# Cross-attention of a fused two-block model: softmax units, query chunks and value products dealt out in another order

## The chip, the core and the metric

The kernel runs on one core of a Trainium2 chip. The metric is device time in microseconds for one execution. The engines that matter are PE (TensorE, matmuls), DVE (VectorE), ACT (ScalarE), POOL (GpSimd) and SP, which only issues weight transfers. Each engine takes its instructions in the order in which the program writes them, and waits on semaphores where it needs another engine's result.

## The reference

A first block of two layers (gated recurrence, sparse attention) is followed by a second block of two layers (convolution, retention, spatial gating, cross-attention, gated feed-forward). The change lies in the second block's cross-attention, which each of its two layers runs once, on 512 tokens, 256 memory rows and a model width of 1024:

```python
def cross_attention(h, mm, wq, wk, wv, wo):
    q = (h @ wq).reshape(B, S, XA_HEADS, XA_HEAD_DIM)      # 4 heads of 256
    k = (mm @ wk).reshape(B, M, XA_HEADS, XA_HEAD_DIM)
    v = (mm @ wv).reshape(B, M, XA_HEADS, XA_HEAD_DIM)
    s = jnp.einsum('bshd,bmhd->bhsm', q, k).astype(jnp.float32) * (XA_HEAD_DIM ** -0.5)
    p = jax.nn.softmax(s, axis=-1).astype(v.dtype)
    o = jnp.einsum('bhsm,bmhd->bshd', p, v).reshape(B, S, D_MODEL)
    return o @ wo
```

## The kernel before

Every float32 product is made of three matmuls on split operands: high by high, low by high, high by low. Weights come in chunks of 128 x 1024 numbers through a ring of four slots: SP loads a chunk into `raw`, ACT rounds it to `whi` (three chunks ahead of its use), POOL subtracts for `wlo`, and PE uses both. Results in PSUM banks are split in the same way: ACT writes the high part, DVE subtracts for the low part and so frees the bank.

`steps_two()` writes out by hand the list of steps of a layer. All engines walk through this one list, each doing its own share of every step, so the list fixes the order of the work on each engine. The steps of the cross-attention are:

- a *query chunk*, `("fm", "xq", i, ..)`: 24 matmuls of 512 columns for 128 of the 1024 columns of q. DVE scales the result into `tA` or `tB`, ACT copies that to `qx8`, DVE subtracts for its low part. Head h needs chunks 2h and 2h+1.
- a *value chunk*, `("tm", "xv0" or "xv1", i, ..)`: 12 matmuls of 512 columns. Four of them fill banks 2 and 7 (`xv1`), and only the last one has its result copied out.
- a *unit*, `("xatt", hh, qt)`: u = 4 hh + qt, 16 in all. On PE it holds `scores(v)`, six matmuls of 256 columns, for those units v that `scored_in(u)` names, and then `probs_turn(u + 1)`, two transposes. So scores run ahead, by as much as `scored_to(u)` says. Between the scores and the transposes of a unit stand DVE's maximum (`greatest`), ACT's exponential and sum (`probs`) and DVE's reciprocal and scaling of `Px` (`shares`). After the transposes, ACT and DVE copy them, split, into `PxT` (`turned` on ACT); this frees the transposes' bank for the unit after the next.
- a *value product*, `("xout", hh)`: 12 matmuls of 512 columns on `PxT` and `vx`.
- an *output chunk*, `("tm", "xw0", i, ..)`: 24 matmuls of 512 columns, the first two on the results of heads 0 and 1, the next two on those of heads 2 and 3.

`groups_two` says which PSUM banks the results of a step take, in turns.

Before the change, query chunks 0 to 3 stand ahead of the scores, chunks 4 to 7 behind units 2, 3, 6 and 7, the four value chunks behind units 0 to 3, and the value product of a head directly behind its last unit (and the chunk there). Units 8 to 15 have no weight chunk between them. Scores run two units ahead up to unit 3, three at unit 4, four from unit 5.

Of the kernel before, what the change touches and what calls it, by code (L numbers as in the profile page):

```python
# [36 lines left out]
TT = T // P  # L37
KD = D // P
# [18 lines left out]
XH, XD = 4, 256  # L57
# [136 lines left out]
def tm(kind, *a, **k):  # L194
    specs = tm_chunks(*a, **k)
    return [("tm", kind, i, len(specs), s) for i, s in enumerate(specs)]
# [186 lines left out]
def steps_two():  # L383
# [27 lines left out]
    xv1 = tm("xv1", "xa_v_2", 512, 512)  # L411
    xq = fm("xq", "xa_q_2", 0, KD)
    s += [("sums", "xa")] + xv0[:2] + [("rows", "xa")] + xq[:2] + xv0[2:3] + xq[2:3] + xv0[3:] + xq[3:4]
    for hh in range(XH):
        for qt in range(TT):
            s += [("xatt", hh, qt)] + (xv1[qt:qt + 1] if hh == 0 else [])
            s += xq[2 + 2 * hh + qt:3 + 2 * hh + qt] if qt >= 2 else []
        s += [("xout", hh)]
    xw1 = tm("xw1", "xa_o_2", 512, 512)
    s += tm("xw0", "xa_o_2", 0, 512) + xw1[:2] + [("turn_low", "ffn")] + xw1[2:]  # L420
    up = [x for f in range(FT) for x in (("fm", "u", f, ("w1_2", 0, KD, f * P, P)), ("fm", "w", f, ("w3_2", 0, KD, f * P, P)))]
# [12 lines left out]
def scored_to(u):  # L434


    return min(u + (2 if u < 4 else 3 if u == 4 else 4), XH * TT - 1)


def scored_in(u):  # L440
    return range(scored_to(u - 1) + 1 if u else 0, scored_to(u) + 1)


def groups_two(step):
    kind = step[0]
# [27 lines left out]
    if kind == "xatt":  # L473
        hh, qt = step[1:]
        return [(("xs", *divmod(u, TT)), (0, 1) if u < 6 else (2, 7, 0, 1)) for u in scored_in(hh * TT + qt)] + [(("xp", hh, qt), (3, 4))]
    if kind == "xout":
        return [(("xo", step[1], i), (5, 6)) for i in range(2)]
    return []


def build(nc, d, out, counts):
# [3 lines left out]
    with ExitStack() as ctx:  # L485
# [175 lines left out]
        ffn = ExitStack()  # L661
# [1116 lines left out]
        def tensor_two(pe, l):  # L1778
# [214 lines left out]
            def probs_turn(u):  # L1993
                name = ("xp", *divmod(u, TT))
                pe.wait_ge(*px_ready.at(l, u + 1))
                turn(name, MT, lambda i: Px[:, u % 4, i * P:(i + 1) * P])

            def step_xatt(step):
                hh, qt = step[1:]
                u = hh * TT + qt  # L2000
                if u == 0:
                    pe.wait_ge(*G.evacuated(("xk", KD - 1), l))
                for v in scored_in(u):
                    scores(v)
                    if v == 1:
                        probs_turn(0)
                if u + 1 < XH * TT:
                    probs_turn(u + 1)

            def step_xout(step):  # L2010
# [4 lines left out]
                for i in range(2):  # L2015
                    name, cols = ("xo", hh, i), slice(hh * XD + i * P, hh * XD + (i + 1) * P)
                    pe.wait_ge(*G.free(name, l))
                    for m in range(MT):
# [7 lines left out]
                     "ret_out": step_ret_out, "ret_turn": step_ret_turn, "sg_w": step_sg_w, "sg_mix": step_sg_mix,  # L2026
                     "sg_turn": step_sg_turn, "mg_turn": step_mg_turn, "xatt": step_xatt, "xout": step_xout}
            for step in steps2:
# [12 lines left out]
        def scalar_two(act, l):  # L2041
# [201 lines left out]
            def turned(u):  # L2243
                hh, qt = divmod(u, TT)
                name = ("xp", hh, qt)
                hi(PxT[:, hh % 2, 0, :, qt * P:(qt + 1) * P], name, G.ps(name)[:, 0:MEM].rearrange("p (m q) -> p m q", m=MT))

            def step_xatt(step):
                hh, qt = step[1:]
                u = hh * TT + qt  # L2250
                for v in scored_in(u):
                    if v == u + 2 or (v > 1 and v == scored_in(u)[0]):
                        turned(u)
                    probs(v)
                if not len(scored_in(u)):
                    turned(u)

            def step_xout(step):
                for i in range(2):
# [4 lines left out]
                     "ret_pair": step_ret_pair, "ret_out": step_ret_out, "ret_turn": step_ret_turn, "sg_w": step_sg_w, "sg_norm": step_sg_norm,  # L2264
                     "sg_turn": step_sg_turn, "mg_turn": step_mg_turn, "xatt": step_xatt, "xout": step_xout}
            for step in steps2:
# [6 lines left out]
        def vector_two(dve, l):  # L2273
# [285 lines left out]
            def shares(u):  # L2559
# [4 lines left out]
                ts(Px[:, u % 4, :], Px[:, u % 4, :], recx[:, c], None, ALU.mult).then_inc(*px_ready.up())  # L2564

            def step_xatt(step):
                hh, qt = step[1:]
                u = hh * TT + qt
                for v in scored_in(u):
                    if v > 1:  # L2570
                        shares(v - 1)
                    greatest(v)
                    if v == 1:
                        shares(0)
                if scored_to(u) == XH * TT - 1 and len(scored_in(u)):
                    shares(XH * TT - 1)
                at = (slice(None), slice(None), slice(qt * P, (qt + 1) * P))
                lo(PxT[:, hh % 2, 1][at], ("xp", hh, qt), PxT[:, hh % 2, 0][at], src=G.ps(("xp", hh, qt))[:, 0:MEM].rearrange("p (m q) -> p m q", m=MT))

            def step_xout(step):  # L2580
                for i in range(2):
# [3 lines left out]
                    else:  # L2585
# [4 lines left out]
                     "ret_out": step_ret_out, "ret_turn": step_ret_turn, "sg_w": step_sg_w, "sg_norm": step_sg_norm,  # L2590
                     "sg_mix": step_sg_mix, "sg_turn": step_sg_turn, "mg_turn": step_mg_turn, "xatt": step_xatt, "xout": step_xout}
            for step in steps2:
# [277 lines left out]
```

## Time and profile before

| what | value |
|---|---|
| time, median of 3 runs | 2967.58 us (2965.24 to 2969.01) |
| span of the profiled execution | 2966.5 us |
| PE busy | 2781.2 us, 94% |
| PE weight loads busy | 2312.4 us, 78% |
| ACT busy | 1283.9 us, 43% |
| DVE busy | 1225.9 us, 41% |
| POOL busy | 1157.0 us, 39% |
| mean granted TensorE clock | 0.971 |

The times are those of whole executions. The profile describes one further execution, whose own time is known only as its span from the first to the last instruction, 2966.5 us; it lies 1.1 us under the median of the timed runs and within their spread. In the rows below, the granted clock (PEclk) is a share of 2.4 GHz: 1.00 is the upper level and 0.50, 1.2 GHz, the lower. Starts are in us from the span's start. A busy time is what an engine worked in a stretch; the rest of the stretch it waited.

### The profile page before, as it was taken

What the parts mean: (1) busy time and instruction counts of PE and PEld (TensorE: products, weight loads), DVE (VectorE), ACT (ScalarE), POOL (GpSimd) and SP (SyncE); (2) the same over time, 40 slices, a digit from 0 to 9 for tenths busy, and PEclk for the clock granted to TensorE, in tenths of its full rate; (3) what the DMA queues carried; (4) which work ended last, traced back from release to release, by engine and by line L of the source; (5) the groups of instructions that cost most, each with busy time, mean ns of one, the idle gap of its engine ahead of it and who ended that gap; (6) DMA issues with size and microseconds to landing.
All of it is one profiled execution on the core that took longest, in us unless ns stands there. A gap on an engine that the chain in (4) does not pass through costs nothing.

```text
span 2966.5 us, 40477 instructions
## 1 busy us (share of the span) xinstructions
PE 2781.2 (94%) x13636; PEld 2312.4 (78%) x13636; DVE 1225.9 (41%) x2186; ACT 1283.9 (43%) x2191; POOL 1157.0 (39%) x537
## 2 busy tenths in 40 slices
PE   8989799998979998999998999999899999999998
PEld 6778668887856886788877888888688787788887
DVE  4766762476585234424222331313443423232132
ACT  4543754554374452444443432424254443253243
POOL 4323344331334442334442444444234453244442
PEclk9999899999989998999999999999899999999999
DMA  5213003321300231233331333333123333233332
GB/s 145 71 45 79 29 14 93 88 68 46 84 22 17 92 109 57 79 93 93 114 107 57 93 93 96 96 100 110 50 82 96 100 111 96 64 93 99 93 94 99
DMA packets 269778, 242.32 MB, mean 82 GB/s; under 512 B 29376, under 2 KB 201600, under 8 KB 269568
## 3 DMA queue, kind: packets, MB, share of 16 engines
q1 hardware_dynamic: 266672, 235.12, 27.1%
q10 hardware_dynamic: 2896, 4.52, 0.5%
q8 instruction: 118, 1.93, 0.3%
q14 instruction: 92, 0.75, 0.1%
HBM read 237.51 MB, written 2.10 MB: 81 GB/s over the span
## 4 chain that ended last, share of the span: by engine, by line
issue 46%; POOL 26%; PE 25%; DVE 1%; ACT 1%; POOLq 0%; DMA 0%; DVEq 0%; ACTq 0%
POOL wlo L2711 24%; PE bank L1899 4%; PE bank L1903 4%; PE bank L1902 4%; PE bank L1837 3%; PE bank L1833 3%; PE bank L1836 3%; PE bank L1788 1%; POOL Ql L2703 0%; PE bank L2020 0%; POOL vv L2703 0%; POOL dE L2703 0%; POOL Kl L2703 0%; POOL At L2703 0%; POOLq L2710 0%
## 5 line engine op out<-in xcount | busy, mean ns | idle before, releaser
L2711 POOL TENSOR_TENSOR wlo<-raw,whi 128x1024 fp32r<-128x1024 f32 (+2 forms) x440 | 1061.3, 2417 | 1637.8 <-ACT whi L2039 1637.6
L2039 ACT CAST whi<-raw 128x1024 fp32r<-128x1024 f32 (+2 forms) x443 | 456.8, 1035 | 700.2 <-PE bank L1899 465.7
L1833 PE MATMUL bank<-xhi,whi 128*128 128x512 f32 x928 | 364.9, 393 | 0.3 <-issue 0.3
L1837 PE MATMUL bank<-xhi,wlo 128*128 128x512 f32 x928 | 363.0, 391 | 0.0
L1836 PE MATMUL bank<-xlo,whi 128*128 128x512 f32 x928 | 362.8, 391 | 0.0
L1899 PE MATMUL bank<-whi,xhi 128*128 128x512 f32 x832 | 328.3, 395 | 9.7 <-POOL wlo L2711 5.7
L1903 PE MATMUL bank<-whi,xlo 128*128 128x512 f32 x832 | 325.8, 392 | 0.0
L1902 PE MATMUL bank<-wlo,xhi 128*128 128x512 f32 x832 | 325.7, 391 | 0.0
L791 PE MATMUL bank<-whi,xhi 128*128 128x512 f32 (+2 forms) x704 | 262.2, 372 | 3.1 <-DVE pT L1418 3.1
L794 PE MATMUL bank<-wlo,xhi 128*128 128x512 f32 (+2 forms) x704 | 257.3, 365 | 0.0
L795 PE MATMUL bank<-whi,xlo 128*128 128x512 f32 (+2 forms) x704 | 257.0, 365 | 0.0
L1833 PEld LDWEIGHTS bank<-xhi,whi 128*128 128x128 f32 x928 | 175.5, 189 | 38.1 <-issue 1.7
L1837 PEld LDWEIGHTS bank<-xhi,wlo 128*128 128x128 f32 x928 | 175.1, 189 | 36.9
L1836 PEld LDWEIGHTS bank<-xlo,whi 128*128 128x128 f32 x928 | 175.4, 189 | 36.0
L1899 PEld LDWEIGHTS bank<-whi,xhi 128*128 128x128 f32 x832 | 157.6, 189 | 43.7 <-POOL wlo L2711 6.6
L1903 PEld LDWEIGHTS bank<-whi,xlo 128*128 128x128 f32 x832 | 157.3, 189 | 33.4
L1902 PEld LDWEIGHTS bank<-wlo,xhi 128*128 128x128 f32 x832 | 157.5, 189 | 31.9
L791 PEld LDWEIGHTS bank<-whi,xhi 128*128 128x128 f32 x704 | 136.0, 193 | 24.5 <-DVE pT L1418 3.6
L795 PEld LDWEIGHTS bank<-whi,xlo 128*128 128x128 f32 x704 | 135.5, 192 | 20.6
L794 PEld LDWEIGHTS bank<-wlo,xhi 128*128 128x128 f32 x704 | 135.9, 193 | 19.2
L2403 DVE TENSOR_TENSOR h<-h,bank 128x512 f32<-128x512 f32 x64 | 44.0, 687 | 249.6 <-PE bank L1903 249.6
L1899 PE MATMUL bank<-whi,gT 128*128 128x512 f32 x352 | 137.3, 390 | 1.6 <-DVE et L2396 1.6
(492 smaller groups left out, 4965.1 us busy)
## 6 DMA issues: line engine op xcount, KB each, us to landing
raw<-in_w_in SPq DMA_DIRECT2D x147, 512.0 KB, 3.7
raw<-in_w SPq DMA_DIRECT2D x132, 512.0 KB, 3.8
raw<-in_w_pg SPq DMA_DIRECT2D x16, 512.0 KB, 3.8
raw<-in_w_o SPq DMA_DIRECT2D x16, 512.0 KB, 3.8
raw<-in_xa_k SPq DMA_DIRECT2D x16, 512.0 KB, 3.9
raw<-in_xa_v SPq DMA_DIRECT2D x16, 512.0 KB, 4.0
raw<-in_xa_q SPq DMA_DIRECT2D x16, 512.0 KB, 4.0
raw<-in_xa_o SPq DMA_DIRECT2D x16, 512.0 KB, 3.8
```

Of the source, the lines that this page charges most:

```text
L791: mm = pe.matmul(o, a, wh, start=(i == 0 and kk_ == 0), stop=False)
L794: pe.matmul(o, a, wl, start=False, stop=False)
L795: mm = pe.matmul(o, b, wh, start=False, stop=(i == n - 1 and kk_ == nk - 1))
L1833: mm = pe.matmul(o, wh, rhs[0][:, k, :], start=(k == 0), stop=False)
L1836: pe.matmul(o, wh, rhs[1][:, k, :], start=False, stop=False)
L1837: mm = pe.matmul(o, wl, rhs[0][:, k, :], start=False, stop=(k == KD - 1))
L1899: mm = pe.matmul(G.ps(name)[:, :], a, wh, start=(i == 0 and kk_ == 0), stop=False)
L1902: pe.matmul(G.ps(name)[:, :], a, wl, start=False, stop=False)
L1903: mm = pe.matmul(G.ps(name)[:, :], b, wh, start=False, stop=(i == n - 1 and kk_ == nk - 1))
L2039: nc.scalar.copy(whi[:, j % SLOTS, 0:nk * cols], raw[:, j % SLOTS, 0:nk * cols]).then_inc(hi_split, 1)
L2403: tt_(at, at, G.ps(name)[:, :], ALU.add).then_inc(*G.empty(name))
L2711: nc.gpsimd.tensor_tensor(wlo[:, s, 0:n], raw[:, s, 0:n], whi[:, s, 0:n].bitcast(F32), ALU.subtract).then_inc(lo_split, 1)
```

## The change

No operation is added or removed. The list of steps is written in another order, and scores run ahead by another rule:

- a step `xfirst` holds the scores of units 0 and 1; it stands behind query chunk 2, ahead of chunk 3. Unit 0 then scores unit 2 first and makes the transposes of units 0 and 1 after that.
- query chunks 3 to 7 stand behind units 0, 2, 4, 7 and 8, value chunks 0 to 3 of `xv1` behind units 1, 3, 6 and 9.
- the value products of heads 0, 1 and 2 stand behind units 5, 10 and 12 (before: 3, 7 and 11). That of head 3 stands between the first and the second output chunk (before: ahead of the first), and takes banks 0 and 1.
- scores run two units ahead up to unit 9, three at unit 10, four from unit 11.
- the transposes use banks 4 and 3 in turn instead of 3 and 4, the scores of units 12 to 15 banks 2, 7, 0 and 1 (before: of units 6 to 15).

```diff
-    s += [("sums", "xa")] + xv0[:2] + [("rows", "xa")] + xq[:2] + xv0[2:3] + xq[2:3] + xv0[3:] + xq[3:4]
-    for hh in range(XH):
-        for qt in range(TT):
-            s += [("xatt", hh, qt)] + (xv1[qt:qt + 1] if hh == 0 else [])
-            s += xq[2 + 2 * hh + qt:3 + 2 * hh + qt] if qt >= 2 else []
-        s += [("xout", hh)]
-    xw1 = tm("xw1", "xa_o_2", 512, 512)
-    s += tm("xw0", "xa_o_2", 0, 512) + xw1[:2] + [("turn_low", "ffn")] + xw1[2:]
+    xw0, xw1 = tm("xw0", "xa_o_2", 0, 512), tm("xw1", "xa_o_2", 512, 512)
+    s += [("sums", "xa")] + xv0[:2] + [("rows", "xa")] + xq[:2] + xv0[2:] + xq[2:3] + [("xfirst",)]
+    between = [xq[3], xv1[0], xq[4], xv1[1], xq[5], ("xout", 0), xv1[2], xq[6], xq[7], xv1[3], ("xout", 1), None, ("xout", 2)]
+    for u in range(XH * TT):
+        s += [("xatt", *divmod(u, TT))] + [x for x in between[u:u + 1] if x]
+    s += xw0[:1] + [("xout", 3)] + xw0[1:] + xw1[:2] + [("turn_low", "ffn")] + xw1[2:]
...
-    return min(u + (2 if u < 4 else 3 if u == 4 else 4), XH * TT - 1)
+    return min(u + (2 if u < 10 else 3 if u == 10 else 4), XH * TT - 1)
...
-    return range(scored_to(u - 1) + 1 if u else 0, scored_to(u) + 1)
+    return range(scored_to(u - 1) + 1 if u else 2, scored_to(u) + 1)
...
-        return [(("xs", *divmod(u, TT)), (0, 1) if u < 6 else (2, 7, 0, 1)) for u in scored_in(hh * TT + qt)] + [(("xp", hh, qt), (3, 4))]
+        return [(("xs", *divmod(u, TT)), (0, 1) if u < 12 else (2, 7, 0, 1)) for u in scored_in(hh * TT + qt)] + [(("xp", hh, qt), (4, 3))]
+    if kind == "xfirst":
+        return [(("xs", 0, u), (0, 1)) for u in range(2)]
     if kind == "xout":
-        return [(("xo", step[1], i), (5, 6)) for i in range(2)]
+        return [(("xo", step[1], i), (5, 6) if step[1] < XH - 1 else (0, 1)) for i in range(2)]
...
             def step_xatt(step):
                 for v in scored_in(u):
-                    if v > 1:
-                        shares(v - 1)
+                    shares(v - 1)
                     greatest(v)
-                    if v == 1:
-                        shares(0)
```

On DVE, this is the program around query chunk 6, before the change. `tA` and `qx8` are the chunk's; `recx` and `Px` are the normalisation of a unit, here of unit 10; `nmx` is the maximum of unit 11.

```order
L2378 SCALAR_TENSOR_TENSOR tA<-bank5,tD 128x512 [waits filled5]
L2379 REGISTER_ALU
L2380 TENSOR_TENSOR qx8<-tA,qx8 128x512 [waits hi_done]
L2561 REGISTER_ALU
L2563 RECIPROCAL recx<-sumx 128x1 [waits emptied2]
L2281 REGISTER_ALU
L2564 TENSOR_SCALAR Px<-Px,recx 128x256 [waits dve_step]
L2557 TENSOR_REDUCE nmx<-bank7 128x1 [waits filled7]
```

And in the changed kernel, at the same query chunk. Here the normalisation is that of unit 9, and the maximum that of unit 10.

```order
L2385 SCALAR_TENSOR_TENSOR tA<-bank5,tD 128x512 [waits filled5]
L2386 REGISTER_ALU
L2387 TENSOR_TENSOR qx8<-tA,qx8 128x512 [waits hi_done]
L2568 REGISTER_ALU
L2570 RECIPROCAL recx<-sumx 128x1 [waits emptied1]
L2281 REGISTER_ALU
L2571 TENSOR_SCALAR Px<-Px,recx 128x256 [waits dve_step]
L2564 TENSOR_REDUCE nmx<-bank0 128x1 [waits filled0]
```

The instructions are the same; the unit whose `Px` is normalised behind the chunk is the one that PE transposes next in the changed kernel (unit 9 in unit 8's step), and the third next in the one before (unit 10, where PE transposes unit 8).

On PE, this is the start of the units before the change: scores of units 0 and 1, transposes of unit 0, scores of unit 2, transposes of unit 1.

```order
L1989 MATMUL bank0<-kx8,qx8 128x256 x5
L1984 REGISTER_ALU
L1989 MATMUL bank1<-kx8,qx8 128x256 [waits emptied1]
L1989 MATMUL bank1<-kx8,qx8 128x256 x5
L1995 ISA
L1786 REGISTER_ALU [waits px_ready]
L1788 MATMUL bank3<-ident,Px 128x128 [waits emptied3]
L1788 MATMUL bank3<-ident,Px 128x128
L1984 REGISTER_ALU
L1989 MATMUL bank0<-kx8,qx8 128x256 [waits emptied0]
L1989 MATMUL bank0<-kx8,qx8 128x256 x5
```

The same place in the changed kernel, whose unit 0 scores unit 2 ahead of both transposes:

```order
L1989 MATMUL bank0<-kx8,qx8 128x256 x5
L1984 REGISTER_ALU
L1989 MATMUL bank1<-kx8,qx8 128x256 [waits emptied1]
L1989 MATMUL bank1<-kx8,qx8 128x256 x5
L1984 REGISTER_ALU
L1989 MATMUL bank0<-kx8,qx8 128x256 [waits emptied0]
L1989 MATMUL bank0<-kx8,qx8 128x256 x5
L1995 ISA
L1788 MATMUL bank4<-ident,Px 128x128 [waits emptied4,px_ready]
L1788 MATMUL bank4<-ident,Px 128x128
```

The scores of unit 2 moved ahead of the first transposes.

On DVE, this is the end of the units in the changed kernel, behind the product of head 1 (its remainders are written to `mmT`): the normalisations of units 14 and 15, the last maximum, and then the copies of the transposes of units 11 and 12.

```order
L2570 RECIPROCAL recx<-sumx 128x1 [waits emptied0]
L2281 REGISTER_ALU
L2571 TENSOR_SCALAR Px<-Px,recx 128x256 [waits dve_step]
L2564 TENSOR_REDUCE nmx<-bank1 128x1 [waits filled1]
L2568 REGISTER_ALU
L2570 RECIPROCAL recx<-sumx 128x1 [waits emptied1]
L2281 REGISTER_ALU
L2571 TENSOR_SCALAR Px<-Px,recx 128x256 [waits dve_step]
L2298 REGISTER_ALU
L2301 TENSOR_TENSOR PxT<-bank3,PxT 128x2x128 [waits hi_done]
L2298 REGISTER_ALU
L2301 TENSOR_TENSOR PxT<-bank4,PxT 128x2x128 [waits hi_done]
```

Before, the product of head 1 stood four units earlier, and the copy of unit 12 behind the product of head 2.

## Rows read from the trace of the kernel before

**Rows 1.** The page, its first line.
```profile
span 2966.5 us, 40477 instructions
```

**Rows 2.** The page, part 4: chain that ended last, shares by engine.
```profile
issue 46%; POOL 26%; PE 25%; DVE 1%; ACT 1%; POOLq 0%; DMA 0%; DVEq 0%; ACTq 0%
```

**Rows 3.** Busy time by stretch; its first line names the columns.
```profile
core 0: us, PE busy (x) PEld busy (x) DVE busy (x) ACT busy (x) POOL busy (x), PEclk, DMA share, GB/s
1514.70:1519.91 5.21, 2.88 (x23) 2.68 (x22) 3.03 (x9) 2.01 (x6) 0.00 (x0) 0.97 0.36 104
1519.91:1524.18 4.27, 4.27 (x14) 3.40 (x13) 1.23 (x4) 1.77 (x4) 2.28 (x1) 0.64 0.00 0
1527.86:1528.71 0.85, 0.85 (x10) 0.85 (x8) 0.00 (x0) 0.00 (x0) 0.85 (x1) 1.00 0.00 0
1536.98:1540.04 3.06, 1.07 (x10) 0.86 (x8) 2.13 (x6) 0.89 (x2) 0.00 (x0) 1.00 0.43 162
1540.04:1544.47 4.43, 4.43 (x14) 3.53 (x14) 1.03 (x3) 2.19 (x4) 2.39 (x1) 0.61 0.00 0
1549.93:1552.65 2.72, 2.72 (x13) 2.25 (x12) 1.83 (x3) 1.21 (x2) 0.00 (x0) 1.00 0.59 188
1552.65:1560.08 7.43, 4.84 (x37) 4.22 (x36) 4.81 (x16) 3.36 (x12) 0.00 (x0) 1.00 0.00 1
1560.08:1567.27 7.19, 7.19 (x27) 5.76 (x27) 1.18 (x4) 1.77 (x5) 2.38 (x1) 0.76 0.13 32
1576.37:1584.86 8.49, 4.55 (x33) 3.70 (x32) 5.99 (x20) 3.90 (x13) 0.00 (x0) 0.97 0.11 42
1584.86:1589.08 4.22, 4.22 (x13) 3.35 (x13) 0.64 (x1) 0.59 (x1) 0.00 (x0) 0.65 0.00 0
1589.08:1592.74 3.66, 1.15 (x7) 0.55 (x6) 2.16 (x6) 1.84 (x5) 0.00 (x0) 1.00 0.00 0
1514.70:1595.61 80.91, 67.55 (x322) 55.75 (x321) 31.71 (x83) 29.60 (x70) 19.09 (x8) 0.92 0.20 59
2467.02:2547.94 80.92, 67.51 (x322) 55.64 (x320) 31.72 (x83) 29.60 (x70) 19.06 (x8) 0.92 0.20 59
1415.50:1418.50 3.00, 2.92 (x13) 2.44 (x14) 0.00 (x0) 1.05 (x1) 1.27 (x1) 1.00 0.82 325
```

**Rows 4.** Timeline of PE behind query chunk 6 (start, duration).
```profile
1567.27 0.88 PE L1989 MATMUL bank<-kx,qx 128*128 128x256 f32 x6
1567.98 0.38 PE L1788 MATMUL bank<-ident,Px 128*128 128x128 f32 x2
```

**Rows 5.** Timeline of DVE and PE behind query chunk 4.
```profile
1538.56 0.69 DVE L2380 TENSOR_TENSOR qx<-tA,qx 128x512 fp32r<-128x512 f32 x1 [0.69 <-ACT qx L2146]
1539.17 0.15 DVE L2563 RECIPROCAL recx<-sumx 128x1 f32<-128x1 f32 x1
...
1539.85 0.53 PE L1788 MATMUL bank<-ident,Px 128*128 128x128 f32 x2 [1.99 <-DVE Px L2564]
```

**Rows 6.** Timeline of ACT (unit 0) and DVE (unit 1) at the start.
```profile
1517.72 0.19 ACT L2240 ACTIVATION_READ_ACCUMULATOR Px<-bank,nmx 128x1 f32 x1
...
1518.60 0.35 DVE L2564 TENSOR_SCALAR Px<-Px,recx 128x256 f32<-128x256 f32 x1
```

**Rows 7.** Timeline behind value chunk 3 (DVE) and behind product 0 (PE).
```profile
1545.29 0.69 DVE L2294 TENSOR_TENSOR vx<-bank,vx 128x512 fp32r<-128x512 f32 x1 [1.00 <-ACT vx L2091]
...
1554.67 0.44 PE L1788 MATMUL bank<-ident,Px 128*128 128x128 f32 x2 [0.43 <-DVE Px L2564]
```

**Rows 8.** Timeline of DVE ahead of product 2, and PE behind it.
```profile
1582.33 0.16 DVE L2563 RECIPROCAL recx<-sumx 128x1 f32<-128x1 f32 x1 [0.30 <-ACT Px L2240]
...
1583.85 0.16 DVE L2563 RECIPROCAL recx<-sumx 128x1 f32<-128x1 f32 x1 [0.63 <-ACT Px L2240]
...
1590.97 0.77 PE L1788 MATMUL bank<-ident,Px 128*128 128x128 f32 x4 [1.51 <-DVE PxT L2294]
```

**Rows 9.** Timeline of PE at another wait, outside the cross-attention's units.
```profile
1415.58 0.49 PE L1899 MATMUL bank<-whi,xhi 128*128 128x512 f32 x1 [1.96 <-DVE xlo L2294]
```

More of the change, by code:

```diff
@@ L1996, in probs_turn, with step_xfirst @@
                 turn(name, MT, lambda i: Px[:, u % 4, i * P:(i + 1) * P])
+            def step_xfirst(step):
+                pe.wait_ge(*G.evacuated(("xk", KD - 1), l))
+                scores(0)
+                scores(1)
             def step_xatt(step):
@@ L2000, in step_xatt @@
                 u = hh * TT + qt
-                if u == 0:
-                    pe.wait_ge(*G.evacuated(("xk", KD - 1), l))
                 for v in scored_in(u):
                     scores(v)
-                    if v == 1:
-                        probs_turn(0)
+                if u == 0:
+                    probs_turn(0)
                 if u + 1 < XH * TT:
@@ L2026, in tensor_two @@
                      "ret_out": step_ret_out, "ret_turn": step_ret_turn, "sg_w": step_sg_w, "sg_mix": step_sg_mix,
-                     "sg_turn": step_sg_turn, "mg_turn": step_mg_turn, "xatt": step_xatt, "xout": step_xout}
+                     "sg_turn": step_sg_turn, "mg_turn": step_mg_turn, "xfirst": step_xfirst, "xatt": step_xatt, "xout": step_xout}
             for step in steps2:
@@ L2246, in turned, with step_xfirst @@
                 hi(PxT[:, hh % 2, 0, :, qt * P:(qt + 1) * P], name, G.ps(name)[:, 0:MEM].rearrange("p (m q) -> p m q", m=MT))
+            def step_xfirst(step):
+                probs(0)
+                probs(1)
             def step_xatt(step):
@@ L2251, in step_xatt @@
                 for v in scored_in(u):
-                    if v == u + 2 or (v > 1 and v == scored_in(u)[0]):
+                    if v == scored_in(u)[0]:
                         turned(u)
@@ L2264, in scalar_two @@
                      "ret_pair": step_ret_pair, "ret_out": step_ret_out, "ret_turn": step_ret_turn, "sg_w": step_sg_w, "sg_norm": step_sg_norm,
-                     "sg_turn": step_sg_turn, "mg_turn": step_mg_turn, "xatt": step_xatt, "xout": step_xout}
+                     "sg_turn": step_sg_turn, "mg_turn": step_mg_turn, "xfirst": step_xfirst, "xatt": step_xatt, "xout": step_xout}
             for step in steps2:
@@ L2564, in shares, with step_xfirst @@
                 ts(Px[:, u % 4, :], Px[:, u % 4, :], recx[:, c], None, ALU.mult).then_inc(*px_ready.up())
+            def step_xfirst(step):
+                greatest(0)
+                greatest(1)
+                shares(0)
             def step_xatt(step):
@@ L2569, in step_xatt @@
                 for v in scored_in(u):
-                    if v > 1:
-                        shares(v - 1)
+                    shares(v - 1)
                     greatest(v)
-                    if v == 1:
-                        shares(0)
                 if scored_to(u) == XH * TT - 1 and len(scored_in(u)):
@@ L2590, in vector_two @@
                      "ret_out": step_ret_out, "ret_turn": step_ret_turn, "sg_w": step_sg_w, "sg_norm": step_sg_norm,
-                     "sg_mix": step_sg_mix, "sg_turn": step_sg_turn, "mg_turn": step_mg_turn, "xatt": step_xatt, "xout": step_xout}
+                     "sg_mix": step_sg_mix, "sg_turn": step_sg_turn, "mg_turn": step_mg_turn, "xfirst": step_xfirst, "xatt": step_xatt, "xout": step_xout}
             for step in steps2:
```

## The prediction

> **What bounds the kernel now.** I read the page first, then the windows, then the timeline. The profiled span is 2966.5 us [rows 1]; the timed runs have a median of 2967.58, so 1.1 us lies outside the span or between executions, and I add differences to the median. The chain [rows 2] gives most of its time to "issue", to POOL's split of weight chunks and to PE's matmuls. PE is fed in order and nearly always has a next matmul, so a change of order can only alter PE's waits and what its clock costs.
>
> The change lies between the last query chunk ahead of the scores and the first output chunk. This stretch occurs once a layer: 80.91 us in the first, 80.92 in the second, with PE busy 67.5 [rows 3]. POOL works 19.1 us of it, so the weight ring isn't the limit. I write S(u), X(u), T(u) for the six score matmuls, the softmax, and the two transposes of unit u (16 units, 4 a head), and C(u) for the split copy of T(u). Work that stays the same: a product takes 2.72 us at full clock (twelve 512-wide matmuls; a value chunk has twelve such too), a query chunk with its 24 twice that, 5.44, a unit without a wait 0.85 (S 0.71, T 0.14) [rows 3, 4].
>
> What isn't work is two things.
>
> - Waits. The unit stretches of one layer take 5.21 (units 0, with S(0) to S(2)), 3 x 0.85 (units 1, 2, 7), 3.06 (unit 3), 7.43 (units 4 to 6), 8.49 (units 8 to 11 and the wait for C(11)), 3.66 (T(13) to T(15)): 30.40 us together [rows 3].
> - Slow spells of PE. After some waits the granted clock falls to its lower level, 1.2 of 2.4 GHz, and comes back after some work. A value chunk then took 4.27 and 4.43 instead of 2.72, a query chunk 7.19 instead of 5.44, a product 4.22 instead of 2.72 [rows 3]: four spells a layer, 6.5 us.
>
> **Where the waits come from.** After query chunk 4, VectorE scales the chunk, waits for ScalarE's copy and subtracts. The chunk's matmuls give way to S(5) at 1536.98; the subtraction begins at 1538.56 and ends 2.27 us after that. Only then does VectorE turn to the normalisation of X(4) (its reciprocal starts 0.08 before the end shown, at 1539.17), and T(4) starts at 1539.85, 2.87 after the chunk, having waited 1.99 [rows 5]. So a unit behind a query chunk costs 3.06 if its own T needs a normalisation queued behind that chunk. This is so where scores run two units ahead. After chunk 6 they run further ahead: S(11) starts at 1567.27 and T(8) at 1567.98 with no wait, because X(8) was normalised long before the chunk [rows 4].
>
> **The change, stretch by stretch (one layer, full clock).** The diff keeps scores two ahead until unit 9 and puts chunks 3 to 7 behind units 0, 2, 4, 7 and 8. VectorE's order shows the normalisation of X(u+1) right behind each query chunk and PE needs it for the T(u+1) in the next unit, as in the measured case. No instruction count changes; DMAs and POOL's splits follow the order of the chunks, which is only more even.
>
> 1. Start, S(0) S(1) S(2) T(0) T(1). S(2) now goes ahead of T(0) (shown with the change), but needs the bank of S(0), which ScalarE frees when its sum is read at 1517.72 + 0.19, 3.21 after the chunk's end at 1514.70. T(1) needs Px of unit 1, ready at 1518.95 [rows 6], so it starts at 4.38. I take 4.55 for the stretch against 5.21: 0.66 gained.
> 2. Units 1, 3, 5, 8, 9, each behind a query chunk: 5 x 3.06 = 15.30.
> 3. Units 2, 4, 7, behind value chunks 0, 1, 2: these leave nothing in VectorE's queue. 3 x 0.85 = 2.55.
> 4. Unit 6, behind the product of head 0. T(5) stood behind this product before and started 2.02 after its end (1554.67 against 1552.65), after two scores [rows 7]. With one score the wait grows, the place is the same: 2.02 + 0.20 = 2.22.
> 5. Unit 10, behind value chunk 3. S(12) and S(13) use banks 2 and 7, which that chunk fills. VectorE's second remainder ended 1.51 after the chunk (1545.98 against 1544.47) [rows 7]. S(13) therefore starts at 1.55, T(11) at 2.26: 2.45.
> 6. Unit 11 is two scores and a transpose: 1.56.
> 7. T(13) needs the bank of T(11), so C(11). VectorE has that behind X(13), X(14) and X(15), and the remainders of product 1. These end 1.51 after the product; one X follows another every 1.52 (reciprocals at 1582.33 and 1583.85), and PE resumed at 1584.86, 1.01 after the last of them, when C(11) was done [rows 3, 8]. That is 1.51 - 0.08 + 2 x 1.52 + 1.01 = 5.48, plus 0.19 for T(13): 5.67 after the product. Less unit 11: 4.11. This wait of about 3.9 us replaces the 2.33 ahead of product 2; it is the only one longer than before.
> 8. T(14) runs at once behind product 2, T(15) needs C(13): 1.89 after the product, as the transpose at 1590.97 [rows 8]. The first output chunk needs the bank of T(14), about 0.3 later. 2.30. The output chunk then hides C(14) and C(15) from product 3, and the two later output chunks hide that product's copies, so that the split costs nothing behind it. Without this cover it would cost the 1.0 us that PE waited before.
>
> Sum: 4.55 + 15.30 + 2.55 + 2.22 + 2.45 + 1.56 + 4.11 + 2.30 = 35.04 against 30.40, **4.64 us more a layer, 9.3 in both**. The terms moved are what matters: four more units behind query chunks cost 4 x 2.21 = 8.8, and the back-to-back units 4 to 6 and 8 to 11, whose own waits disappear, give back about half.
>
> **The clock.** The place of the spells can't be read off. Waits of 2.33, 1.99, 1.88 and 2.33 us had one behind them; 1.51 did not, nor did 1.96 us at 1415.58, where the clock stayed at 1.00 [rows 3, 9]. That is four in six. The changed block has eight waits over 1.5 us a layer (1.66, five of 1.99, 3.9, 1.8), so 5 spells; but with waits every 6 to 11 us part of each spell falls on waiting, where it costs nothing. I price one at 1.4, under the 1.50 to 1.75 of [rows 3], so 7.0 against 6.5: 0.5 a layer, 1 us. Bounds: three a layer (4.2, so 4.6 less over both layers) and all eight at 1.6 (12.8, so 12.6 more).
>
> Total 9.3 + 1.0 = 10.3: **2978 us**. The bounds of the clock alone give 2972 and 2989.5.
>
> The Trainium skill, "TensorE: Matmul & The Clock Gate", section "Why this matters for your kernels", advises to keep idle gaps between bursts of matmuls below a length that of all these waits only the one ahead of T(13) exceeds. The trace of before does not agree: 1.99 us of waiting had a value chunk at a granted clock of 0.61 behind it [rows 3, 5].
>
> **Rivals.**
>
> - *Short waits cost no clock here* (the skill page's rule above is this case). Then one spell of 1.5 a layer stays, behind the 3.9 us, and 5 a layer of the old 6.5 are given back: 9.3 - 10 = -0.7, 2967 us, no change. For it: 1.96 us at 1415.58 without a spell. Against it: four of the block's five waits had one, in both layers. 8%. Milder forms (two or three spells) come out within 0.2% as well: 5% more.
> - *Every wait has a spell*: 9.3 + 12.6, 2989.5. For it: 4 in 5 within the block. 10%.
> - *Faster: the query chunk's tail is hidden.* If T(u+1) behind a query chunk did not wait for the chunk's remainder, the five units would cost 0.85 each: 35.04 - 11.0 = 24.0, 6.4 less than before, and with the spell count down to two or three, 3 more: 18 to 20 less over both layers, 2948. It decides once the wait falls under 1.99 - 4.64/5 = 1.06 us. For it: T(8) at 1567.98. Against it: that unit had scores three ahead, the changed ones have two, and T(4) under the same order waited 1.99 in both layers. 6%.
> - *The change moves waits without adding any*: the back-to-back units were as dear as assumed but one of terms 4, 5, 7 is too high by over 1.5 us. Then +6 or less. 5%, counted with no change.
>
> **How the numbers follow.** My forecast has 66%. 0.2% of the median, 5.9 us, is about what a measurement of this kernel can tell from no change. Slower by more takes in the forecast and the second rival, 0.76. The faster case has 0.06, the two of no change 0.18 (13% and 5%). For the range I leave out the faster case and the lower half of the no-change cases below, and the last two spells (1.6 each) above: 2970 to 2987, some 8 in 10.
>
> **What the changed profile would show.** Five waits of about 2.0 us a layer in front of a transpose, released by VectorE's Px, each behind a query chunk (before: one); one of 3.5 to 4.1 us released by PxT in front of T(13); no wait in front of product 3; the start-up stretch 0.5 to 0.8 shorter. From S(0) to the first output chunk, with product 3 added and query chunk 3 taken off so that the same work is compared, it would take 85 to 87 us instead of 80.9. I'd be wrong if Px came in time behind the query chunks (then the queue order is read wrongly), or if the number of slow spells left three to eight a layer.

## The result and the profile after

| | us, median (lowest to highest) |
|---|---|
| before | 2967.28 (2965.24 to 2969.01), 4 runs |
| changed | 2984.94 (2982.11 to 2989.80), 4 runs |
| changed : before | 1.0063, 95% interval 1.0049 to 1.0076 |

The changed kernel is slower by 17.7 us. When it was timed again beside other kernels it had 2982.39 against 2967.62, 14.8 us and a ratio of 1.0047 [1.0031, 1.0064]. Its first profiled execution is the slowest of all of them, 2989.80.

The page's first line and its chain, which answer to [rows 1, 2]:

```profile
span 2987.9 us, 40473 instructions
...
issue 46%; POOL 26%; PE 26%; DVE 1%; ACT 1%; POOLq 0%; DMA 0%; DVEq 0%; ACTq 0%
```

The chain doesn't tell where the time went. The windows do; they answer to [rows 3]. The columns are busy time and instructions of each engine, the granted clock of PE and the DMA load.

```profile
core 0: us, PE busy (x) PEld busy (x) DVE busy (x) ACT busy (x) POOL busy (x), PEclk, DMA share, GB/s
1516.14:1520.74 4.60, 2.94 (x24) 2.57 (x22) 3.32 (x9) 1.75 (x6) 0.00 (x0) 1.00 0.38 111
1526.29:1529.37 3.08, 1.09 (x10) 0.89 (x8) 2.16 (x6) 0.89 (x2) 0.00 (x0) 1.00 0.56 156
1529.37:1533.78 4.41, 4.41 (x14) 3.50 (x13) 0.83 (x3) 1.81 (x4) 2.36 (x1) 0.61 0.00 0
...
1557.12:1561.56 4.44, 4.44 (x15) 3.49 (x13) 1.00 (x2) 1.15 (x3) 0.00 (x0) 0.62 0.00 0
1561.56:1563.85 2.29, 1.06 (x10) 0.85 (x8) 1.44 (x5) 0.86 (x2) 0.00 (x0) 1.00 0.00 0
...
1576.27:1581.80 5.53, 5.53 (x26) 4.59 (x25) 0.24 (x1) 1.55 (x3) 2.40 (x1) 1.00 0.12 6
...
1587.96:1590.20 2.24, 1.93 (x15) 1.73 (x15) 1.45 (x4) 0.97 (x3) 0.92 (x1) 1.00 0.21 16
1593.05:1598.78 5.73, 2.15 (x18) 1.91 (x16) 3.72 (x12) 2.25 (x7) 0.00 (x0) 0.95 0.00 0
1598.78:1602.95 4.17, 4.17 (x14) 3.29 (x13) 0.60 (x1) 0.59 (x1) 0.00 (x0) 0.66 0.02 4
...
1516.14:1613.47 97.33, 78.98 (x369) 64.75 (x368) 33.09 (x85) 31.92 (x73) 23.89 (x10) 0.93 0.20 60
2474.92:2574.83 99.91, 81.33 (x369) 66.56 (x368) 33.10 (x85) 31.98 (x73) 23.85 (x10) 0.90 0.19 58
```

The last two rows are the whole block of each layer, from S(0) to the end of product 3. Without query chunk 3 and the first output chunk, which lie inside it now (2 x 5.44), they are 86.45 and 89.03, against 80.91 and 80.92 before: 5.5 and 8.1 us more. The first row is the start, the second a unit behind a query chunk, the third the value chunk behind that unit, at a granted clock of 0.61.

PE's waits in the first layer, from the timeline (start, length, engine, line, operation, and in brackets the wait and its releaser):

```profile
1519.40 0.98 PE L1989 MATMUL bank<-kx,qx 128*128 128x256 f32 x6 [1.66 <-ACT Px L2243]
1529.15 0.43 PE L1788 MATMUL bank<-ident,Px 128*128 128x128 f32 x2 [1.99 <-DVE Px L2571]
...
1563.66 0.43 PE L1788 MATMUL bank<-ident,Px 128*128 128x128 f32 x2 [1.23 <-DVE Px L2571]
...
1589.24 0.98 PE L1989 MATMUL bank<-kx,qx 128*128 128x256 f32 x6 [0.31 <-DVE vx L2301]
1598.44 0.69 PE L1788 MATMUL bank<-ident,Px 128*128 128x128 f32 x2 [3.58 <-DVE PxT L2301]
1604.84 0.44 PE L1788 MATMUL bank<-ident,Px 128*128 128x128 f32 x2 [1.51 <-DVE PxT L2301]
```

The wait of 1.99 stands five times in each layer (in the first at 1529.15, 1543.03, 1556.90, 1575.98 and 1584.66), where before it stood once, at [rows 5]. What VectorE does ahead of the first of them:

```profile
1527.86 0.69 DVE L2387 TENSOR_TENSOR qx<-tB,qx 128x512 fp32r<-128x512 f32 x1 [0.68 <-ACT qx L2149]
1528.47 0.15 DVE L2570 RECIPROCAL recx<-sumx 128x1 f32<-128x1 f32 x1
1528.66 0.35 DVE L2571 TENSOR_SCALAR Px<-Px,recx 128x256 f32<-128x256 f32 x1
```

This is how an in-order queue shows itself. The reciprocal and the scaling have no bracket: their data had been there (ScalarE had read the sum of unit 2 at 1521.27, seven us earlier, in the timeline). They stood behind the chunk's subtraction, and that waited 0.68 for ScalarE's copy of the chunk. PE resumes at 1529.15, when `Px` is done.

### The profile page after: what moved, and what is told of

Read it like the earlier page. It is cut to its first block, busy times and chain, and to the rows that moved or that the text cites. A ratio compares the mean times of both kernels' runs of the same rounds, so it can differ in the third digit from the quotient of the medians.

```text
span 2987.9 us, 40473 instructions
## 1 busy us (share of the span) xinstructions
PE 2794.4 (94%) x13636; PEld 2322.8 (78%) x13636; DVE 1228.5 (41%) x2186; ACT 1284.5 (43%) x2191; POOL 1156.2 (39%) x537
## 4 chain that ended last, share of the span: by engine, by line
issue 46%; POOL 26%; PE 26%; DVE 1%; ACT 1%; POOLq 0%; DMA 0%; DVEq 0%; ACTq 0%
POOL wlo L2720 23%; PE bank L1899 4%; PE bank L1902 4%; PE bank L1903 4%; PE bank L1837 3%; PE bank L1836 3%; PE bank L1833 3%; PE bank L1788 1%; PE bank L2023 0%; POOL vv L2712 0%; POOL dE L2712 0%; POOL Ql L2712 0%; POOL Kl L2712 0%; POOL At L2712 0%; POOLq L2719 0%
```

## The experiments

Each was timed beside the kernel before; "block" is the stretch of the two windows above, less 10.88, unless the text says that it is the one of [rows 3].

### Normalise a unit ahead of the chunk's tail

The changed kernel, with X(v) put right behind the maximum of unit v, so that no normalisation is left for the next step's queue.

```diff
                 shares(0)
+                shares(1)
...
                 for v in scored_in(u):
-                    shares(v - 1)
                     greatest(v)
-                if scored_to(u) == XH * TT - 1 and len(scored_in(u)):
-                    shares(XH * TT - 1)
+                    shares(v)
```

> The changed kernel, with VectorE normalising Px of a unit in the same step as its maximum, so ahead of the query chunk's two operations instead of behind them. Same order on PE and ScalarE, nothing left out. Theory 1 (the normalisation queued behind the chunk makes PE wait): the ten waits of 1.99 us and the two of 1.23 in front of a transpose go, 10 x 2.2 + 2 x 1.4 = 25 us, and with them most of the slow spells behind them (six in the profiled execution, 1.7 each, 10 us): 2985 - 35 = 2950, range 2945 to 2958. Rival (the new places of the chunks cost by themselves, through banks, the ring or PE's own order): it stays above 2975.

Measured: 2947.31 (2943.26 to 2955.91) against 2967.09, ratio 0.9937 [0.9922, 0.9952]. Windows of this kernel's two blocks and of query chunk 3 in the first, and then, from its timeline, the two longest waits that are left behind unit 9:

```profile
1510.78:1593.99 83.21, 75.29 (x369) 63.04 (x368) 34.54 (x85) 31.55 (x73) 23.91 (x10) 0.94 0.24 70
2453.60:2534.06 80.46, 72.56 (x369) 61.11 (x368) 34.51 (x85) 31.45 (x73) 23.93 (x10) 0.98 0.24 72
...
1515.40:1522.53 7.13, 7.13 (x26) 5.75 (x25) 0.94 (x4) 1.76 (x4) 2.37 (x1) 0.77 0.20 58
```

```profile
1568.39 1.70 PE L1989 MATMUL bank<-kx,qx 128*128 128x256 f32 x12 [1.66 <-DVE vx L2301]
...
1577.85 0.69 PE L1788 MATMUL bank<-ident,Px 128*128 128x128 f32 x2 [3.11 <-DVE PxT L2301]
```

No wait is released by VectorE's `Px` any more, and the blocks are 72.3 and 69.6 instead of 86.5 and 89.0. Of these 33.6 us some 10 are slow spells: three are left in both blocks (query chunk 3 above, and product 2 at 5.27 and 4.19), where the changed kernel had nine. The rest is waits. The place of two small operations in VectorE's queue is worth some 35 us: it turns the change from 15 to 18 us slower into 20 us faster. It also rules out that the new places of the chunks cost that time by themselves, since they are the same here. The rival "faster: the query chunk's tail is hidden" is thereby a true account of what would happen if `Px` came in time; it doesn't in the changed kernel.

### The copy of unit 11 ahead of the last normalisations

The changed kernel, with C(11) moved ahead of the normalisations and the last maximum of its step. Everything else stays; `copies()` is the line `lo(PxT...)`, put into a function.

```diff
+                if u == 11:
+                    copies()
                 for v in scored_in(u):
                     shares(v - 1)
                     greatest(v)
                 if scored_to(u) == XH * TT - 1 and len(scored_in(u)):
                     shares(XH * TT - 1)
-                lo(PxT[:, hh % 2, 1][at], ("xp", hh, qt), ...)
+                if u != 11:
+                    copies()
```

> The changed kernel, with VectorE's copy of the transposes of unit 11 moved ahead of the last three normalisations; nothing else changed. If the wait of 3.58 us in front of the transposes of unit 13 comes from that copy's place in VectorE's queue, it falls to about 1.0 us (the normalisation of unit 13 then ends it), unit 14's transposes wait some 0.8 instead of 0, so 1.8 us a layer and perhaps a slow spell of 1.5 to 2.5 as well: 2979, range 2976 to 2983. If the tail is bound by the last normalisations themselves, no change: 2985.

Measured: 2973.66 (2968.91 to 2978.39) against 2967.09, 1.0019 [1.0010, 1.0029], below the range expected. T(13) and T(15) in its timeline:

```profile
1587.97 0.43 PE L1788 MATMUL bank<-ident,Px 128*128 128x128 f32 x2 [0.61 <-DVE Px L2571]
...
1592.93 0.44 PE L1788 MATMUL bank<-ident,Px 128*128 128x128 f32 x2 [1.22 <-DVE PxT L2301]
```

The 3.58 us ahead of T(13) fell to 0.61, 3.0 us a layer or 6 in both. The blocks are 80.45 and 83.71, though, 11.3 less in both together. Most of the missing 5 is clock. Product 2, which took 4.17 and 5.18 behind the long wait, takes 3.08 in both layers, 3.2 less. Another 1.6 is the value chunk behind unit 1 in the first layer, 2.81 instead of 4.41, although the wait of 1.99 ahead of it is still there. The cause named in the expectation holds; its size doesn't. The wait fell to 0.61 and not to 1.0, unit 14's transposes did not wait 0.8 in exchange, and the spell behind the wait went with it.

### The split of the output projection alone

The kernel before, with only product 3 put between the output chunks and its banks changed as in the diff.

```diff
-        s += [("xout", hh)]
+        s += [("xout", hh)] if hh < XH - 1 else []
...
-    s += tm("xw0", "xa_o_2", 0, 512) + xw1[:2] + [("turn_low", "ffn")] + xw1[2:]
+    xw0 = tm("xw0", "xa_o_2", 0, 512)
+    s += xw0[:1] + [("xout", XH - 1)] + xw0[1:] + xw1[:2] + [("turn_low", "ffn")] + xw1[2:]
```

> The kernel before, with one part of the change alone: product 3 stands between the first and second output chunk (banks 0 and 1, transposes on banks 4 and 3). The wait of 1.00 us in front of product 3 goes, but the first output chunk now waits for the copy of unit 14's transposes: it would start about 0.4 us earlier than product 3 did. 0.8 us over both layers: 2966.5, no change that can be told. If the whole 1.00 us and the 1.51 ahead of it could be hidden, 5 us less: 2962.

Measured: 2965.53 (2963.42 to 2978.01) against 2967.09, 0.9995 [0.9982, 1.0008]. The first output chunk starts 3.25 us behind product 2, where product 3 had started 3.66 behind it. No difference can be told; the split costs nothing that shows.

### Query chunks in pairs

The changed kernel, with query chunks 4 and 5, and 6 and 7, each put behind one unit, so that a layer has three units behind query chunks and not five. Empty places keep the rest in order.

```diff
-    between = [xq[3], xv1[0], xq[4], xv1[1], xq[5], ("xout", 0), xv1[2], xq[6], xq[7], xv1[3], ("xout", 1), None, ("xout", 2)]
+    between = [xq[3:4], xv1[:1], xq[4:6], xv1[1:2], xv1[2:3], [("xout", 0)], [], [], xq[6:], xv1[3:], [("xout", 1)], [], [("xout", 2)]]
```

> The changed kernel, with query chunks 4 and 5 both behind unit 2 and 6 and 7 both behind unit 8; value chunk 2 behind unit 4 instead of 6; nothing left out. Theory 1: three Px waits of 1.99 us a layer instead of five, but units 5 to 8 stand with less between them and wait about 1 us more in sum: 3.4 us less a layer, 6.8 in both, and two slow spells a layer fewer at most (0 to 7 us): 2975, range 2970 to 2980. If what matters is the number of query chunks between the units and not where they stand, 2985.

Measured: 2969.19 (2966.87 to 2976.59) against 2967.09, 1.0013 [1.0003, 1.0023]. This is just below the range expected. There are three waits of 1.99 a layer, and in place of the other two, besides the 1.23 behind product 0 that was there already, two of 0.38 where units now stand side by side. The blocks are 81.07 and 79.92, 14.5 less in both together. Some 6 of that are waits; the other 8.5 are clock, since four spells are left of nine (the value chunk behind unit 1 at 4.42 in each layer, product 2 at 5.27 and 4.13). The number of units behind query chunks is what makes the change slow: with three of them it is within 0.2% of before.

### The change again

The changed kernel once more, beside the next three, to see how far its executions differ.

> The changed kernel once more, unchanged. The first profile of it was its slowest execution (2989.8 of 2982.1 to 2989.8), and its first layer's scores start 1.4 us later than those of before although a query chunk of 5.4 us comes later, so 6.9 us were lost ahead of the changed steps. If that is the clock falling at other moments in executions of the same program, this profile shows the same waits in the two blocks to 0.1 us, another number of slow spells in them (three to six a layer), and another start of the first scores (1509 to 1516 us); median 2983 to 2986. If the change itself costs something ahead of the block, the scores start at 1516 again.

Measured: 2982.39 (2979.97 to 2988.45) against 2967.62, 1.0047 [1.0031, 1.0064]. Its two blocks in the profile:

```profile
1508.40:1605.75 97.35, 79.00 (x370) 64.71 (x368) 33.10 (x85) 32.01 (x73) 23.87 (x10) 0.93 0.19 60
2467.03:2566.99 99.96, 81.34 (x369) 66.65 (x368) 33.10 (x85) 31.95 (x73) 23.87 (x10) 0.90 0.19 58
```

The blocks repeat to within 0.05 us, and so does their clock, 0.93 and 0.90. The span is 2980.1, 13.6 over [rows 1], and the blocks are 13.7 over theirs, so the whole difference lies in them. The first block starts at 1508.40 here and at 1516.14 in the first profile: those 7.7 us lie ahead of the block, in the part that the change doesn't touch. From 250 to 500 us, for one, the granted clock was 0.93 here and 0.90 there. The expectation had another number of slow spells in the blocks; it was the same nine, behind the same waits.

### S(2) ahead of T(0) alone

The kernel before, with the transposes of unit 0 behind all three scores.

```diff
                 for v in scored_in(u):
                     scores(v)
-                    if v == 1:
-                        probs_turn(0)
+                if u == 0:
+                    probs_turn(0)
```

> The kernel before, with one part of the change alone: scores of unit 2 ahead of the transposes of unit 0. The start stretch takes 4.60 us instead of 5.21, so 1.2 us less over both layers: 2966, not to be told from no change. If a wait for the bank of unit 0 held more than that up, slower.

Measured: 2964.75 (2960.90 to 2974.93) against 2967.62, 0.9990 [0.9979, 1.0000]. Its start, and value chunk 3, from the windows:

```profile
1520.62:1525.12 4.50, 2.84 (x23) 2.54 (x22) 3.22 (x9) 1.65 (x6) 0.00 (x0) 1.00 0.42 123
...
1543.83:1546.66 2.83, 2.83 (x14) 2.33 (x14) 0.88 (x3) 2.10 (x4) 1.19 (x1) 1.00 0.00 0
```

4.50 against 5.21. The blocks of [rows 3] went down further, to 77.37 and 77.44, because two spells a layer are gone. The value chunk behind the start took 2.84, behind a wait of 1.66 and not 2.33. Value chunk 3 took 2.83 and 2.86 instead of 4.43, although the wait of 1.99 ahead of it is what it was. Yet in this execution the first block started 5.9 us later than in the profile of before, so little of the gain reached its end.

### Early normalisation in the kernel before

The kernel before, with the queue order of the first experiment.

```diff
+                if u == 0:
+                    greatest(0)
+                    greatest(1)
+                    shares(0)
+                    shares(1)
                 for v in scored_in(u):
                     if v > 1:
-                        shares(v - 1)
-                    greatest(v)
...
+                        greatest(v)
+                        shares(v)
```

> The kernel before, with VectorE normalising Px in the step of its maximum, as in the run that did this to the changed kernel. The 1.99 us wait behind query chunk 4 and the 0.43 behind product 0 go (2.6 a layer), but units 4 to 6 and 8 to 11 follow one another directly, so each copy now waits for a normalisation more: about 1.2 us more ahead of unit 7's transposes and 0.5 a unit in units 8 to 11. Sum near zero: 2966, range 2961 to 2970. If the early normalisation is good by itself wherever the chunks stand, it falls by 7 us or more, to 2960 or less.

Measured: 2964.52 (2959.17 to 2978.54) against 2967.62, 0.9985 [0.9969, 1.0001]. Three stretches, from the windows: unit 3, units 4 to 6, and units 8 to 11 with the wait behind them.

```profile
1539.53:1540.38 0.85, 0.85 (x9) 0.85 (x8) 0.65 (x1) 0.00 (x0) 0.00 (x0) 1.00 0.56 171
1551.40:1560.04 8.64, 4.73 (x38) 4.33 (x36) 5.24 (x17) 3.68 (x13) 0.00 (x0) 0.98 0.03 12
1576.16:1585.20 9.04, 4.54 (x34) 3.69 (x32) 5.57 (x18) 3.91 (x13) 0.00 (x0) 1.00 0.06 22
```

Unit 3 lost its wait, 3.06 to 0.85, but the units that stand back to back took 8.64 instead of 7.43 and 9.04 instead of 8.49 [rows 3]: there PE consumes units as fast as VectorE makes them, and the early normalisation stands ahead of a copy that PE waits for. In the profile the blocks of [rows 3] are shorter all the same, 77.30 and 77.24: unit 3 gave 2.21, and value chunk 3 (2.86) and product 2 (2.85 behind a wait of 1.48) had no spell. Of these 7.3 us the median shows 3.1, and the interval takes in no change. So early normalisation alone gains little, if anything; in the changed kernel it was worth 35. It gains where a chunk stands between units, which is what the change brings; and the change loses without it.

### Both orders

The first experiment and, in every step, the copy ahead of the normalisation.

```diff
                 for v in scored_in(u):
-                    shares(v - 1)
                     greatest(v)
-                if scored_to(u) == XH * TT - 1 and len(scored_in(u)):
-                    shares(XH * TT - 1)
...
                 lo(PxT[:, hh % 2, 1][at], ("xp", hh, qt), ...)
+                for v in scored_in(u):
+                    shares(v)
```

> The changed kernel, with the early normalisation (as in the first experiment) and every unit's copy ahead of the normalisations of its step. The 3.1 us wait in front of unit 13 falls to about 1.2, with perhaps a slow spell less: 2947 - 4 = 2943, range 2938 to 2947. If unit 13 is bound by the last normalisations instead, it stays at 2947.

Measured: 2938.70 (2937.20 to 2941.12) against 2967.62, 0.9899 [0.9882, 0.9915]. A block, from the windows:

```profile
1509.97:1586.65 76.68, 71.10 (x369) 59.96 (x368) 34.68 (x85) 31.47 (x73) 23.95 (x10) 1.00 0.26 76
```

and what is left of waits behind unit 9, from the timeline:

```profile
1566.00 1.70 PE L1989 MATMUL bank<-kx,qx 128*128 128x256 f32 x12 [1.66 <-DVE vx L2301]
...
1573.08 0.44 PE L1788 MATMUL bank<-ident,Px 128*128 128x128 f32 x2 [0.74 <-DVE PxT L2301]
...
1578.03 0.44 PE L1788 MATMUL bank<-ident,Px 128*128 128x128 f32 x2 [1.51 <-DVE PxT L2301]
```

The clock is 1.00 over the whole block, in both layers: with fewer waits the spells are all gone. The block is 65.8, against 80.9 before and 86.5 and 89.0 with the change as it was.

### The waits filled with matmuls

The changed kernel, where the scores ahead of the five late transposes are computed three times over, each time from zero. The result is the same; PE has work while it would wait.

```diff
-                for i in range(2):
+                for i in 3 * (0, 1) if u - 2 in (1, 3, 5, 8, 9) else (0, 1):
```

> The changed kernel, in which the scores behind each of the five query chunks (units 3, 5, 7, 10 and 11, scored in the steps of units 1, 3, 5, 8 and 9) are computed three times over into the same bank, 12 more matmuls of 0.12 us; the last time gives the result. PE works 1.42 us of what was a wait of 1.99, and the transposes behind it start when they did, 2.87 us after the chunk, since VectorE takes the maximum only after the normalisation. So the stretches keep their 3.06 us and only the clock can differ. If waiting is what lowers the clock, the slow spells behind these waits (three a layer in both profiles, 1.7 us each) go: 2983 - 10 = 2973, range 2970 to 2977. If the spells come from elsewhere, or short waits cost no clock, 2983.

Measured: 2968.66 (2964.77 to 2988.15) against 2967.93, 1.0000 [0.9984, 1.0017], which is below the range expected. From the windows, its two blocks, the first filled unit, and the value chunk behind that:

```profile
1519.30:1611.87 92.57, 81.41 (x430) 68.47 (x428) 33.09 (x85) 31.88 (x73) 23.94 (x10) 0.98 0.20 63
2474.41:2567.87 93.46, 82.30 (x429) 69.19 (x428) 33.09 (x85) 31.92 (x73) 23.93 (x10) 0.96 0.20 63
...
1529.46:1532.55 3.09, 2.54 (x22) 2.34 (x20) 2.17 (x6) 0.89 (x2) 0.00 (x0) 1.00 0.54 158
1532.55:1535.35 2.80, 2.80 (x14) 2.33 (x13) 0.82 (x3) 1.81 (x4) 1.18 (x1) 1.00 0.03 6
```

The unit behind the chunk takes what it took, 3.09 against 3.08, and PE now waits 0.55 of it; `Px` is as late as ever. But the value chunk takes 2.80 at a granted clock of 1.00 where it took 4.41 at 0.61. All seven spells behind the filled waits are gone, in both layers; the two behind T(13), whose wait was not filled, stay (product 2 at 4.39 and 5.11). The two blocks together are 11.2 us shorter, by work that nobody needs. The profiled execution was a long one all the same, 2982.82, since its first block began 10.9 us later than in the repeated profile. The experiment tells the two parts of the loss apart: the late `Px` costs PE its wait, and the idling costs it the clock behind. A single spell that is missing would not show this, since one of the seven was missing in the experiment with the copy too, with its wait in place; seven of seven are hard to put down to that.

### Other banks for the scores of units 12 and 13

The kernel with both orders, with the banks of the last scores in another order, so that S(12) and S(13) don't take those that value chunk 3 has just filled.

```diff
-        return [(("xs", *divmod(u, TT)), (0, 1) if u < 12 else (2, 7, 0, 1)) for u in scored_in(hh * TT + qt)] + ...
+        return [(("xs", *divmod(u, TT)), (0, 1) if u < 12 else (0, 1, 2, 7)) for u in scored_in(hh * TT + qt)] + ...
```

> The kernel with early normalisation and early copies, in which the scores of units 12 to 15 take banks 0, 1, 2 and 7 in this order instead of 2, 7, 0 and 1. The scores of units 12 and 13 no longer need the banks that value chunk 3 has just filled. The wait of about 1.5 us for VectorE's second remainder in unit 10 goes if nothing else holds it: 3 us less over both layers, 2936. If the normalisations or copies behind the value chunk hold the transposes as long, 2939.

Measured: 2935.15 (2932.91 to 2936.86) against 2967.93, 0.9884 [0.9869, 0.9899]. Its first block, from the windows:

```profile
1507.66:1582.40 74.74, 70.81 (x370) 60.04 (x368) 34.51 (x85) 31.25 (x73) 23.98 (x10) 1.00 0.26 78
```

1.94 us less than the one with both orders. The wait of 1.66 ahead of S(12) is gone: unit 10 runs from 1561.85 to 1563.42 without one. This is the lowest median of all versions, 33 us under the kernel before. Four executions stand behind it, and its interval reaches that of both orders, so that the gain over them rests on the blocks.

## Why the prediction was right, and where a term was off

The change made the kernel slower, by 17.7 us where 10.3 were forecast, and by the mechanism that was forecast. The terms for the waits came out to 0.2 us. What was too small is the price of the clock, with some small terms that were left out, and the first measurement lies above the repeated one by what the blocks don't explain.

**The terms of the sum**, from the windows of the changed kernel, per layer:

| term | predicted | layer 1 | layer 2 |
|---|---|---|---|
| 1, start | 4.55 | 4.60 | 4.60 |
| 2, five units behind query chunks | 15.30 | 15.40 | 15.38 |
| 3, units 2, 4, 7 | 2.55 | 2.56 | 2.54 |
| 4, unit 6 | 2.22 | 2.29 | 2.29 |
| 5, unit 10 | 2.45 | 2.24 | 2.52 |
| 6 and 7, unit 11, the wait, T(13) | 5.67 | 5.73 | 5.72 |
| 8, T(14), T(15) | 2.30 | 2.22 | 2.22 |
| sum | 35.04 | 35.04 | 35.27 |

Against 2 x 30.40 that is 9.5 us more in both layers, where 9.3 were predicted. The mechanism is the one named: `Px` behind the query chunk's subtraction, five times a layer, shown by the first experiment, which removes all five waits with one change of VectorE's order. It rested on a single case before the change [rows 5], which the changed kernel repeats at 1.99 every time. In term 7 the queue behind product 1 was read rightly too: 3.58 against "about 3.9", with C(11) as its cause, shown by the second experiment. In term 5 S(12) had to wait as well, in the first layer: it started 0.51 us after the last matmul of value chunk 3 had started, where the matmuls of that chunk are 0.23 apart. With other banks (the last experiment) this wait is gone. One wait was read too long, the last one: 1.8 us ahead of T(15), where it is 1.51 as in [rows 8]; the term that holds it came out right.

**The clock.** This term was mis-sized. The prediction had five spells a layer at 1.4 us, 14.0 in both, +1.0 over before. The profile has four in the first layer (chunks of 4.41 and 4.42, products of 4.44 and 4.17, 6.56 over 2.72 each) and five in the second (9.27 over), 15.8 in both: +2.8. The number was nearly right and the price too low, 1.76 a spell. That part of a spell would fall on waiting, and cost nothing there, did not show: seven of the nine spells were whole, at 1.69 to 1.72, and product 2 of the second layer took 5.18.

**What the sum left out.** The blocks rose by 13.65; waits and spells make 12.3. The other 1.3 are in small parts. The query chunks and the first output chunk, each behind a unit now, took 5.53 to 5.58 instead of 5.44, which is some 1.1 more than before in both layers; before, chunks 4 and 5 stood behind a value chunk and took 5.43 and 5.46, and chunk 7, behind a unit, 5.54. The rest is S(12)'s 0.3 in the first layer. No run isolates what a chunk pays for the unit in front of it.

The sign that the prediction gave for the block, 85 to 87 us, holds for the first layer (86.45) and fails for the second (89.03), whose fifth spell and longer product 2 it didn't have.

So the block gives 2967.58 + 13.65 = 2981, 3 over the forecast, and the repeated measurement's 2982.39 is near it. The first measurement's median has 2.5 more. Its profiled execution has 7.8 more than the repeated one by its span, and 7.7 of them lie ahead of the block, in steps that the change leaves alone. Where the 2.5 of the median lie no profile shows. Executions of one program differ there: in the twelve profiles, whose steps ahead of the block are the same, the first block began between 1507.7 and 1519.3 us (with 5.44 taken off where query chunk 3 stands ahead of it).

**The rivals.**

- *Short waits cost no clock*: falls. The waits of 1.99 us at 1529.15, 1543.03 and 1556.90 each had a chunk or product at 0.61 or 0.62 behind them, and the filled waits took this away. By the Trainium skill, "TensorE: Matmul & The Clock Gate", section "Why this matters for your kernels", such gaps would have been short enough; the trace of this kernel does not agree. It isn't a rule that every such wait has a spell either: behind the one at 1575.98 query chunk 7 took 5.53 at 1.00.
- *Every wait has a spell*: falls for the same reason; nine spells of the sixteen that it needed. The time lies between the forecast and this rival's 2989.5 through the price, not the number.
- *Faster*: falls for the changed kernel, but its account of the machine holds. It had 11.0 us a layer from five units at 0.85, and 2948 in all; the first experiment, which makes it so, measured 2947.31.
- *Waits moved without adding any*: falls with the table above.

**What stays open** is the place of each spell. The same program put them in the same places in the block, as its repetition shows; but what decides between the wait at 1556.90 and the one at 1575.98 no run here tells. A change far from a wait can take its spell away or bring it back: with the split alone, value chunk 3 took 2.84 in the first layer and 4.44 in the second, behind a wait of 1.99 in both. So the number of spells could be forecast only roughly, and nine against ten was in part luck.

## What to carry to other kernels

Look at what an in-order engine has in its queue ahead of the one small operation that the bottleneck engine waits for: here 0.5 us of VectorE work behind a chunk's tail cost 2 us of TensorE's time ten times over, and a move by a few lines was worth 35 us. Early normalisation in the kernel before gained nothing clear of the noise (3.1 us by the medians), and the dealing out of the chunks without it lost 15 to 18; a schedule and the queue order under it have to be changed together, and tried together before one is thrown out. Price a wait with what the clock takes behind it: in the changed kernel seven of ten waits of 1.99 us took another 1.7.

## What the hardware showed that was not expected

- Matmuls without a purpose saved time. Sixty more of them a layer, in five waits of 1.99 us, took 11.2 us off the two blocks and some 14 off the median (2968.66 against 2982.39), since the granted clock stayed at 1.00 behind these waits.
- A spell can last through a whole product. This is the window of the changed kernel that holds product 2 of the second layer:

```profile
2559.13:2564.31 5.18, 5.18 (x15) 4.00 (x13) 0.69 (x1) 0.59 (x1) 0.00 (x0) 0.51 0.00 0
```

  It took 5.18 us at 0.51, behind a wait of 3.57; the first layer's took 4.17 at 0.66, behind 3.58.
- Once the block's waits were few (1.67, 1.66, 0.74 and 1.51 us with both orders), its clock never fell, in either layer. In the kernel before, with waits of 2.33, 1.99 and 1.88, it fell four times a layer. A short wait isn't safe by itself, though: with early normalisation alone, the wait of 1.67 at the start had query chunk 3 at 7.13 us and 0.77 behind it in the first layer, and at 5.56 in the second.
- A shorter block need not show in the time of one execution: with S(2) first the two blocks were 7.0 us shorter and the span only 1.2, because the first block began 5.9 us later than in the profile of before, though nothing in front of it had changed. The median was 2.9 lower; where the rest of the 7.0 went in it no profile shows.
